# Two small loads and one matmul group of a two-block transformer kernel: packed loads issued early from GpSimd's queue become strided loads issued later from ScalarE's queue, and half-width matmuls become full-width

## The chip, the cores and the metric

One Trainium2 chip, one core. The kernel is one program that keeps its own weights, activations and intermediate results on that core. The metric is the device time of one execution in microseconds (us); lower is better. Times of matrices below are read from one profiled execution.

## The reference

A batch of one sequence of 256 rows with 2048 features goes through two transformer blocks, all in float32. The first block has gated linear attention, forgetting attention and attention to a memory, then an MLP. The second one, on which the change bears, begins with one wide projection and a sparse attention whose keys and values are first compressed, and with a pooling mixer beside it:

```
h = rms_norm_2(x, ln_mix_pre); z = h @ w_in                  # [256, 7728]
# compressed keys (kv = 0) and values (kv = 1), windows of 32 rows, stride 16, so 15 windows:
blk  = raw[:, idx] + cmp_pe[kv]                              # cmp_pe: [2, 32, 64]
kc/vc = gelu(flat(blk) @ cmp_w1[kv]) @ cmp_w2[kv]            # w1: [2048, 128], w2: [128, 64]
...
# pool mixer, per group g with trailing window w in (2, 4, 8, 16):
y = trailing_mean(u_g, w) - u_g ;  y = y @ w_pool[g] ;  y * pool_scale
```

Then come the merge of both branches, a cross-attention and a gated feed-forward, each with a norm behind it. The trailing mean of the pool mixer is computed as a product with a banded 256 x 256 matrix: column s1 of the band has entries only in the rows s0 with s1 - w < s0 <= s1 (less the identity), so the lower row block (rows 128 to 255) has nothing but zeros in columns 0 to 127.

## The kernel before

Each large product is made from float32 weights that are split in two parts. The work is cut into weight chunks of 1 MB (512 rows x 512 columns), which SyncE's queue (SP) loads into four slots `raw[:, c % SLOTS]`, line L336. A chunk is two halves q. For each half ScalarE rounds the weights into `whi` (function `hi`, line L563, engine ACT), VectorE makes the rest `wlo = raw - whi` (function `lo`, L1250, engine DVE), and TensorE (PE) makes 12 matmuls of 512 columns with them (function `half`, lines L2195, L2196, L2197) that stream into `ps_a`. `whi` and `wlo` have four places each.

The order is held by counters: `hi(q)` waits for `pe_half` >= q - 3 (TensorE is done with half q - 4), `lo(q)` waits for `hi_done`, `half(q)` waits for `lo_done`, and SP's load of chunk c + 4 waits for `lo_done` of chunk c's second half. So ScalarE may be up to four halves ahead of TensorE, and no more.

All other work of a stage is written by hand between the halves of the same engine program. In the second block's first projection (segment `in2`) each engine runs `for n in range(8, LAST2)`: one half, then `sparse(n)`, which holds what that engine does for the sparse attention and the pool mixer at half n. Halves 0 to 7 stand before the loop, mixed with the turned rows of the norm (`hi_group("n4", ...)`); behind them ScalarE has `square_sums(3)` (lines L670, L675: sums of squares of the 256 rows and a square root), and then the loop begins with `hi(q0 + 8)`.

Other places that matter:

- `pet` (the position embeddings `cmp_pe`) and `cw2` (the second compression weights, the first of them twice) are needed by VectorE's `windows` at n = 21 (L1891, writes `xpe`) and by TensorE after it (L2627, L2629). Both are loaded by one DMA each from GpSimd's queue (POOL), L1173 and L1174, from arrays that the host has laid out (`cmp_pe_t`, `cmp_w2_t`), near the start of the kernel. All their DMAs count on the semaphore `ld["cmp"]`.
- SP loads the first compression weights `cw1`, two DMAs of L418, when TensorE has done four halves of `in2`.
- At n = 68 TensorE multiplies `proj2` with `band` into `ps_b` (L2666): 8 values of x, 2 row blocks b. Row block 1 is multiplied with the columns 128 to 255 of its band alone. At n = 71 there is a product of the same form with `wpool` (L2675), of 16 matmuls with 256 columns. ScalarE and VectorE copy `ps_b` out to `yt` at n = 72.

The last chunk of the projection is a narrow one (`tail2`, 48 columns wide), loaded by one DMA of 2048 short rows.

Of the kernel before, what the change touches and what calls it, by code (L numbers as in the profile page):

```python
# [26 lines left out]
P = 128  # L27
S = 256
SB = S // P
# [26 lines left out]
NSA_H, NSA_G, HD2 = 16, 4, 64  # L56
# [3 lines left out]
NU = NGL + 3 * NSA_H  # L60
# [5 lines left out]
CMP_LEN, CMP_STRIDE = 32, 16  # L66
# [46 lines left out]
def hybrid_blocks_kernel(nc, a, c_base, c_bands, out):  # L113
    es = ExitStack()
    with es:
# [27 lines left out]
        proj2 = sb("proj2", [P, SB, IN2])  # L143
# [74 lines left out]
        band = sb("band", [P, SB, 4, S], at=free2 + 6144)  # L218
        wpool = sb("wpool", [P, 4, 2, S], at=free2 + row2 + 6144)
        pet = sb("pet", [P, 2, CMP_LEN // 2])  # L220
        cw2 = sb("cw2", [P, 3, HD2])
# [20 lines left out]
        ps_b = es.enter_context(nc.psum_tensor("ps_b", [P, 4 * NT], F32))  # L242
# [310 lines left out]
        def _(act):  # L553
# [102 lines left out]
            def square_sums(n):  # L656

                if n in (0, 1, 4):
                    for j in range(4):
                        act.wait_ge(norm_loaded[2 if n == 4 else n][j], 16)  # L660
                elif n == 2:
                    act.wait_ge(evicted, seg["mlp"][2])
                elif n == 3:
                    act.wait_ge(d_add, 64)
                else:
                    act.wait_ge(post_done, 8 * (n - 4))
                to = junk if n < 2 else junk_mix if n < 4 else junk3
                src = norms[n]
                for b in range(SB):
                    ins = nc.scalar.activation(to[:], src[:, b], ACT.Square, accum_out=s_sq[:, b:b + 1])  # L670
                    if b == 0:
                        link(ins)
                ins.then_inc(n_sq, 1)
                act.wait_ge(n_var, n + 1)
                nc.scalar.activation(s_std, s_var, ACT.Sqrt).then_inc(n_std, 1)  # L675
# [276 lines left out]
            hi_group("n4", 3, xhi)  # L952
            some("in2", 6, 8)
            square_sums(3)

            def branch_exps(x, t):
                act.wait_ge(nb["max"], 2 * x + t + 1)
# [193 lines left out]
        @block.gpsimd  # L1151
        def _(pool):
            def load_rows(n, rows_, src):
                for j in range(4):
                    c = slice(j * NT, (j + 1) * NT)
                    pool.dma_start(rows_[:, :, c], a[src][0].rearrange("(b p) d -> p b d", p=P)[:, :, c]).then_inc(norm_loaded[n][j], 16)

            def load_flat(n, src):
                for j in range(4):
                    c = slice(4 * j, 4 * j + 4)  # L1160
                    pool.dma_start(FLAT[n][0][:, c], a[src][:, c]).then_inc(flat_loaded[n][j], 16)

            pool.wait_ge(flat_loaded[0][1], 16)
            load_rows(0, mem_rows, "mem")

            pool.wait_ge(flat_lo, 8)
            load_flat(1, "x_t")
            pool.wait_ge(pe_half, 8)
            load_rows(1, h, "x")
            pool.wait_ge(pe_half, 16)  # L1170
            pool.dma_start(base[:, P:], c_base[:, P:]).then_inc(ld["base"], 16)

            pool.dma_start(pet[:], a["cmp_pe_t"]).then_inc(ld["cmp"], 16)  # L1173
            pool.dma_start(cw2[:], a["cmp_w2_t"]).then_inc(ld["cmp"], 16)  # L1174

            G = nc.gpsimd


            normed = (proj1[:, :, FQ:FQ + 512], proj1[:, :, FK:FK + 512], mkv[:, :, 0:512], proj1[:, :, MQ:MQ + 512])
            pool.wait_ge(hn["rstd"], 1)  # L1180
            for n, v in enumerate(normed):
                for b in range(SB):
                    rows_ = v[:, b].rearrange("p (h d) -> p h d", d=HD)
                    ins = G.tensor_tensor(rows_, rows_, s_hrstd[:, 8 * n + 4 * b:8 * n + 4 * b + 4].unsqueeze(2).to_broadcast([P, 4, HD]), ALU.mult)
                if n % 2:
                    ins.then_inc(hn["rows"], 1)

            pool.wait_ge(pe_half, seg["wout"][1])

            def distance(l):  # L1190
                w = LEVELS_ALL[l]
                if l >= 2:
                    pool.wait_ge(gla["q"], l - 1)
                    pool.wait_ge(gla["k"], l - 1)
                else:
                    pool.wait_ge(gla["b"], 1)
                v = gbt[:].rearrange("p x (m t) -> p (x m) t", t=2 * w)
                G.tensor_tensor(ge[:, l % 2].rearrange("p x (m t) -> p (x m) t", t=2 * w), v,
                                v[:, :, w - 1:w].to_broadcast([P, 4 * S // (2 * w), 2 * w]), ALU.subtract).then_inc(gla["d"], 1)

            distance(0)
            G.memset(gke[:], 0.0).then_inc(gla["zero"], 1)
            pool.wait_ge(gla["zero"], 1)
            for l in range(8):
                w = LEVELS_ALL[l]
                if l < 7:
                    distance(l + 1)
                pool.wait_ge(gla["e"], l + 1)
                if l >= 2:
                    pool.wait_ge(gla["s"], l - 1)  # L1210
                first = [t.rearrange("p x (m t) -> p (x m) t", t=2 * w)[:, :, 0:w] for t in (gke[:, l % 2], gkt[:], ge[:, l % 2])]
                G.tensor_tensor(*first, ALU.mult).then_inc(gla["k"], 1)


            pool.wait_ge(fx["rstd"], 1)
            pool.wait_ge(gate_done, 2)
            fox_mix = mix[:, :, FOX_AT:FOX_AT + 512]
            for b in range(SB):
                G.tensor_tensor(fox_mix[:, b].rearrange("p (h d) -> p h d", d=HD), fox_o[:, b].rearrange("p (h d) -> p h d", d=HD),
                                s_orstd[:, 16 * b + 8:16 * b + 12].unsqueeze(2).to_broadcast([P, 4, HD]), ALU.mult).then_inc(fx["over"], 1)  # L1220
            for b in range(SB):
                pool.wait_ge(fx["over"], b + 1)
                ins = G.tensor_tensor(fox_mix[:, b], fox_mix[:, b], proj1[:, b, FG:FG + 512], ALU.mult)
            ins.then_inc(fx["mixed"], 1)


            pool.wait_ge(t_ps, sum(QUADS["y1"]))
            load_rows(2, mix, "mem_2")
            pool.wait_ge(n_sq, 5)
            load_flat(2, "mem_2_t")  # L1230
# [3 lines left out]
        def _(dve):  # L1234
# [662 lines left out]
            def sparse(n):  # L1897
# [4 lines left out]
                    V.memset(kcbd[:], 0.0).then_inc(ns["zero"], 1)  # L1902
                if n == 21:
                    dve.wait_ge(ns["tk"], 1)
                    dve.wait_ge(ld["cmp"], 16 * 2)
                    windows(0)
                if n == 22:
                    windows(1)
# [272 lines left out]
        def _(pe):  # L2181
# [414 lines left out]
            def sparse(n):  # L2596
# [63 lines left out]
                if n == 68:  # L2660
                    pe.wait_ge(nb["y"], 1)
                    pe.wait_ge(evicted, seg["in2"][2] + 8)
                    pe.wait_ge(band_loaded, 16)
                    for x in range(8):
                        for b in range(SB):
                            ins = mm(ps_b[:, x * S + b * P:(x + 1) * S], proj2[:, b, NU + x * P:NU + (x + 1) * P],  # L2666
                                     band[:, b, x // 2, b * P:S], start=b == 0, stop=b == SB - 1)
                    ins.then_inc(ns["yps"], 1)
                if n == 71:
                    pe.wait_ge(ns["ysb"], 2)  # L2670
# [127 lines left out]


_INS = ["x", "mem", "w_in", "gla_a_w2", "fox_f_b", "w_mem_kv", "w_out", "w_up", "w_down", "mem_2", "ln_mix_post_2", "ln_x_post_2",  # L2800
        "ln_ffn_post_2", "w_in_2", "cmp_w1_2", "w_pool_2", "w_br_attn_2", "w_br_pool_2", "w_mix_out_2",
        "w_xq_2", "w_xkv_2", "w_xo_2", "w_gate_2", "w_up_2", "w_down_2"]


# [4 lines left out]
def laid_out(inputs, index):  # L2809

    flat = {n + "_t": np.asarray(inputs[n])[0].reshape(S, KB, P).transpose(2, 1, 0) for n in ("x", "mem", "mem_2")}
    flat["gains_t"] = np.concatenate([np.asarray(inputs[n]).reshape(-1, P) for n in _GAINS]).T
    table = np.concatenate([np.asarray(inputs["rel_bias_2"])[HEAD_ORDER], np.full((NSA_H, 1), NEG, np.float32)], 1)
    flat["bias"] = table[:, index].transpose(1, 0, 2)
    heads = np.array(HEAD_ORDER)
    kv = 1024 + (np.array(KIND_ORDER)[:, None] * 256 + np.arange(256)).ravel()
    q = (heads[:, None] * HD2 + np.arange(HD2)).ravel()
    gl = NGL + (heads[:, None] * 3 + np.arange(3)).ravel()
    flat["w_in_2"] = np.asarray(inputs["w_in_2"])[:, :, np.concatenate([kv, q, gl, np.arange(NU, IN2)])]
    flat["w_br_attn_2"] = np.asarray(inputs["w_br_attn_2"])[:, q]  # L2820
    flat["cmp_pe_t"] = np.asarray(inputs["cmp_pe_2"])[0].reshape(2, CMP_LEN // 2, P).transpose(2, 0, 1)
    flat["cmp_w2_t"] = np.asarray(inputs["cmp_w2_2"])[0][[0, 0, 1]].transpose(1, 0, 2)
    return {n: np.ascontiguousarray(v, np.float32) for n, v in flat.items()}


# [20 lines left out]
```

## Time and profile before

| | |
|---|---|
| time, median of 3 runs | 2561.34 us (2560.51 to 2563.33) |
| the profiled execution's own time | 2561.34 us |
| its span, first to last instruction | 2559.5 us |
| TensorE matmul busy | 2492.3 us (97%) |
| TensorE weight load busy | 2175.4 us (85%) |
| VectorE busy | 1570.6 us (61%) |
| ScalarE busy | 1209.5 us (47%) |
| GpSimd busy | 61.5 us (2%) |
| share of TensorE in the chain that ended last | 92% |
| mean granted TensorE clock | 0.988 |

The span is 1.84 us shorter than the execution's own time; that execution is the median one. A busy share is an average over stages. The chain that ended last is followed back from the last instruction, at each step to what released it; work that stands in it sets the time. "PEld" is TensorE's weight load, which runs beside its matmuls. "SPq" and "ACTq" rows are DMA issues on the sequencers of SyncE and ScalarE; their duration is the time for which the sequencer was held by the issue.

### The profile page before, as it was taken

To read this page: it belongs to the slowest core of one execution; us is meant where nothing else is said; L and a number is where in the kernel's file an instruction comes from. 1 tells how busy PE (TensorE), PEld (TensorE's weight loads), DVE (VectorE), ACT (ScalarE), POOL (GpSimd) and SP (SyncE) were. 2 spreads that over 40 slices of the span, in tenths; PEclk is the share of its full clock that TensorE was granted. 3 is DMA by queue.
4 is the path that set the end of the run, shared out by engine and by line. 5 is a ranking of instruction groups with operands and counts; after the bars stand their busy time and mean duration, and the time that the engine had idled before them with its cause. 6 is when DMAs were issued, how large, how long until landed. Compare 5 with 4: busy or idle time off the path is not lost.

```text
span 2559.5 us, 31690 instructions
## 1 busy us (share of the span) xinstructions
PE 2492.3 (97%) x12062; PEld 2175.4 (85%) x12062; DVE 1570.6 (61%) x1999; ACT 1209.5 (47%) x1516; POOL 61.5 (2%) x56
## 2 busy tenths in 40 slices
PE   8999988999999999999999999999899999999997
PEld 7888877888888888888888788888788888888886
DVE  6555777656565655566555666766555555555556
ACT  6444454544444444545344545565454444444443
POOL 1000240000000000000000000000000000000000
PEclk9999979999999999999999999999899999999999
DMA  9776405556565656556563445675356666666653
GB/s 369 217 209 198 150 1 191 188 197 202 192 210 185 212 185 208 190 204 228 175 205 132 155 133 196 206 270 183 130 197 198 199 203 202 199 200 203 203 197 115
DMA packets 244526, 488.72 MB, mean 191 GB/s; under 512 B 11928, under 2 KB 13240, under 8 KB 243672
## 3 DMA queue, kind: packets, MB, share of 16 engines
q1 hardware_dynamic: 240576, 470.42, 56.1%
q0 software_dynamic: 3104, 11.79, 1.2%
q10 hardware_dynamic: 760, 5.34, 0.5%
q8 instruction: 57, 0.93, 0.1%
q14 instruction: 29, 0.24, 0.0%
HBM read 485.42 MB, written 2.10 MB: 190 GB/s over the span
## 4 chain that ended last, share of the span: by engine, by line
PE 92%; DVE 3%; ACT 2%; issue 1%; DMA 1%; SPq 0%; DVEq 0%; ACTq 0%
PE ps_a L2195 24%; PE ps_a L2196 24%; PE ps_a L2197 24%; PE ps_b L2196 5%; PE ps_b L2197 5%; PE ps_b L2195 5%; DMA raw<-in_w_mem_kv 1%; PE ps_b L2501 1%; PE ps_b L2260 1%; DVE wlo L1250 1%; PE ps_b L2575 0%; ACT whi L563 0%; PE ps_b L2565 0%; DVE h L1435 0%; ACT prob L962 0%
## 5 line engine op out<-in xcount | busy, mean ns | idle before, releaser
L1250 DVE TENSOR_TENSOR wlo<-raw,whi 128x1024 fp32r<-128x1024 f32 x880 | 1067.8, 1222 | 727.2 <-ACT whi L563 726.1
L563 ACT CAST whi<-raw 128x1024 fp32r<-128x1024 f32 (+1 forms) x884 | 916.0, 1045 | 1065.0 <-PE ps_a L2197 829.4
L2195 PE MATMUL ps_a<-whi,xhi 128*128 128x512 f32 x2016 | 773.0, 383 | 8.8 <-DVE wlo L1250 6.3
L2196 PE MATMUL ps_a<-wlo,xhi 128*128 128x512 f32 x2016 | 766.9, 380 | 0.0
L2197 PE MATMUL ps_a<-whi,xlo 128*128 128x512 f32 x2016 | 766.4, 380 | 0.0
L2195 PEld LDWEIGHTS ps_a<-whi,xhi 128*128 128x128 f32 x2016 | 383.0, 190 | 67.1 <-issue 10.6
L2197 PEld LDWEIGHTS ps_a<-whi,xlo 128*128 128x128 f32 x2016 | 383.0, 190 | 54.0
L2196 PEld LDWEIGHTS ps_a<-wlo,xhi 128*128 128x128 f32 x2016 | 383.1, 190 | 52.2
L2195 PE MATMUL ps_a<-whi,x2hi 128*128 128x512 f32 x640 | 246.0, 384 | 11.5 <-DVE wlo L1250 11.5
L2196 PE MATMUL ps_a<-wlo,x2hi 128*128 128x512 f32 x640 | 243.7, 381 | 0.0
L2197 PE MATMUL ps_a<-whi,x2lo 128*128 128x512 f32 x640 | 243.5, 381 | 0.0
L2195 PEld LDWEIGHTS ps_a<-whi,x2hi 128*128 128x128 f32 x640 | 121.7, 190 | 29.3 <-issue 11.0
L2197 PEld LDWEIGHTS ps_a<-whi,x2lo 128*128 128x128 f32 x640 | 121.7, 190 | 17.2
L2196 PEld LDWEIGHTS ps_a<-wlo,x2hi 128*128 128x128 f32 x640 | 121.8, 190 | 16.6
L2195 PE MATMUL ps_b<-whi,uhi 128*128 128x512 f32 x352 | 133.6, 380 | 0.0
L2197 PE MATMUL ps_b<-whi,ulo 128*128 128x512 f32 x352 | 133.5, 379 | 0.0
L2196 PE MATMUL ps_b<-wlo,uhi 128*128 128x512 f32 x352 | 133.5, 379 | 0.0
L2195 PE MATMUL ps_a<-whi,muhi 128*128 128x512 f32 x272 | 103.4, 380 | 0.0
L2197 PE MATMUL ps_a<-whi,mulo 128*128 128x512 f32 x272 | 103.2, 379 | 0.0
L2196 PE MATMUL ps_a<-wlo,muhi 128*128 128x512 f32 x272 | 103.2, 379 | 0.0
L2196 PE MATMUL ps_b<-wlo,muhi 128*128 128x512 f32 x240 | 91.0, 379 | 0.0
L2197 PE MATMUL ps_b<-whi,mulo 128*128 128x512 f32 x240 | 91.0, 379 | 0.0
(327 smaller groups left out, 1957.2 us busy)
## 6 DMA issues: line engine op xcount, KB each, us to landing
raw<-in_w_in SPq DMA_DIRECT2D x108, 1024.0 KB, 5.3
raw<-in_w_up SPq DMA_DIRECT2D x108, 1024.0 KB, 5.3
raw<-in_w_down SPq DMA_DIRECT2D x108, 1024.0 KB, 5.1
raw<-in_w_gate SPq DMA_DIRECT2D x44, 1024.0 KB, 5.0
raw<-in_w_out SPq DMA_DIRECT2D x16, 1024.0 KB, 5.1
raw<-in_w_mix_out SPq DMA_DIRECT2D x16, 1024.0 KB, 5.7
raw<-in_w_br_attn SPq DMA_DIRECT2D x8, 1024.0 KB, 5.0
raw<-in_w_br_pool SPq DMA_DIRECT2D x8, 1024.0 KB, 5.0
```

The lines of the kernel that those rows point to most:

```text
L563: return nc.scalar.copy(o, i)
L1250: return V.tensor_tensor(wlo[:, q % 4], raw[:, c % SLOTS, 2 * j:2 * j + 2], whi[:, q % 4].bitcast(F32), ALU.subtract).then_inc(lo_done, 1)
L2195: mm(o, x0, m0, start=first and j == 0, stop=False)
L2196: mm(o, x0, m1, start=False, stop=False)
L2197: ins = mm(o, x1, m0, start=False, stop=last and j == len(kbs) - 1)
L2260: ins = nc.tensor.transpose(o[:, m * P:(m + 1) * P], src[:, b, (kb + m) * P:(kb + m + 1) * P], ident)
L2501: ins = nc.tensor.transpose(ps[:, (b * 4 + j) * P:(b * 4 + j + 1) * P], src[:, b, j * P:(j + 1) * P], ident)
```

## The change

Two things are changed.

1. `pet` and `cw2` are no longer loaded by GpSimd's queue, and the host makes no packed arrays. ScalarE's queue loads them from the reference's own arrays, behind `square_sums(3)` and before `hi(q0 + 8)`. `pet` takes four DMAs, one for each kv and each parity t of the row l: 64 partitions (the feature d) with 16 single float32 each, whose source addresses are 64 floats x 2 apart along l and 1 apart along d. `cw2` takes three DMAs of 128 partitions with 64 contiguous floats. VectorE's wait at n = 21 is for 7 DMAs in place of 2.
2. The band product at n = 68 multiplies row block 1 with all 256 columns of its band, in place of the last 128.

```diff
@@ scalar program, behind the first tile of in2
             some("in2", 6, 8)
             square_sums(3)
+            for kv in range(2):
+                for t in range(2):
+                    act.dma_start(pet[t * HD2:(t + 1) * HD2, kv], a["cmp_pe_2"][0, kv].rearrange("(l t) d -> t d l", t=2)[t],
+                                  allow_slow_non_contiguous=True).then_inc(ld["cmp"], 16)
+            for n, kv in enumerate((0, 0, 1)):
+                act.dma_start(cw2[:, n], a["cmp_w2_2"][0, kv]).then_inc(ld["cmp"], 16)
@@ gpsimd program
             pool.dma_start(base[:, P:], c_base[:, P:]).then_inc(ld["base"], 16)
 
-            pool.dma_start(pet[:], a["cmp_pe_t"]).then_inc(ld["cmp"], 16)
-            pool.dma_start(cw2[:], a["cmp_w2_t"]).then_inc(ld["cmp"], 16)
-
@@ vector program, sparse(n)
                 if n == 21:
                     dve.wait_ge(ns["tk"], 1)
-                    dve.wait_ge(ld["cmp"], 16 * 2)
+                    dve.wait_ge(ld["cmp"], 16 * 7)
                     windows(0)
@@ tensor program, sparse(n), n == 68
                         for b in range(SB):
-                            ins = mm(ps_b[:, x * S + b * P:(x + 1) * S], proj2[:, b, NU + x * P:NU + (x + 1) * P],
-                                     band[:, b, x // 2, b * P:S], start=b == 0, stop=b == SB - 1)
+                            ins = mm(ps_b[:, x * S:(x + 1) * S], proj2[:, b, NU + x * P:NU + (x + 1) * P], band[:, b, x // 2],
+                                     start=b == 0, stop=b == SB - 1)
@@ host
-    flat["cmp_pe_t"] = np.asarray(inputs["cmp_pe_2"])[0].reshape(2, CMP_LEN // 2, P).transpose(2, 0, 1)
-    flat["cmp_w2_t"] = np.asarray(inputs["cmp_w2_2"])[0][[0, 0, 1]].transpose(1, 0, 2)
```

(The list of inputs gains `cmp_pe_2` and `cmp_w2_2`.)

## Rows read from the trace of the kernel before

**Rows 1.** The profile's page: engines, and the chain that ended last by engine.

```profile
PE 2492.3 (97%) x12062; PEld 2175.4 (85%) x12062; DVE 1570.6 (61%) x1999; ACT 1209.5 (47%) x1516; POOL 61.5 (2%) x56
...
PE 92%; DVE 3%; ACT 2%; issue 1%; DMA 1%; SPq 0%; DVEq 0%; ACTq 0%
```

**Rows 2.** The chain in order of time: start us, length us, what (band, then wpool group).

```profile
1372.61 5.24 PE ps_b L2666 x32
...
1385.62 6.91 PE ps_b L2675 x32
```

**Rows 3.** ScalarE's timeline from 1174 to 1192 us: start, length, instruction [idle before].

```profile
1178.03 1.05 ACT L563 CAST whi<-raw 128x1024 fp32r<-128x1024 f32 x1 [0.95 <-PE ps_a L2197]
1178.98 1.91 ACT L670 ACTIVATE junk_mix<-h 128x2048 f32<-128x2048 f32 x1
...
1183.24 0.20 ACT L675 ACTIVATE small<-small 128x2 f32<-128x2 f32 x1 [0.24 <-DVE small L1340]
1183.35 1.98 ACT L563 CAST whi<-raw 128x1024 fp32r<-128x1024 f32 x2
1185.80 1.05 ACT L563 CAST whi<-raw 128x1024 fp32r<-128x1024 f32 x1 [0.46 <-PE ps_a L2197]
1188.38 1.05 ACT L563 CAST whi<-raw 128x1024 fp32r<-128x1024 f32 x1 [1.54 <-PE ps_a L2197]
```

**Rows 4.** VectorE's timeline, 1184 to 1190 us, and its first use of `pet`.

```profile
1184.48 3.62 DVE L1250 TENSOR_TENSOR wlo<-raw,whi 128x1024 fp32r<-128x1024 f32 x3 [0.84 <-ACT whi L563]
1188.33 1.41 DVE L1849 TENSOR_SCALAR proj<-ps_a,small 128x512 f32<-128x512 f32 x2 [0.23 <-PE ps_a L2197]
...
1216.51 2.73 DVE L1891 TENSOR_TENSOR xpe<-ps_b,pet 64x240 f32<-64x240 f32 x8
```

**Rows 5.** ScalarE's timeline, 70 to 76 us: two DMA issues and what follows.

```profile
70.98 0.20 ACT L675 ACTIVATE small<-small 128x2 f32<-128x2 f32 x1 [0.24 <-DVE small L1340]
70.99 0.34 ACTq L771 DMA_DIRECT2D gw<-in_gla_a_w  x1
71.37 0.57 ACTq L772 DMA_DIRECT2D fbias<-in_fox_f_b  x1
72.04 2.94 ACT L563 CAST whi<-raw 128x1024 fp32r<-128x1024 f32 x3 [0.85 <-issue]
```

**Rows 6.** SyncE's queue, 1180 to 1190 us: the issues around the `cw1` loads.

```profile
1180.36 0.37 SPq L336 DMA_DIRECT2D raw<-in_w_in  x1
1180.93 4.71 SPq L418 DMA_DIRECT2D cw<-in_cmp_w  x2
1186.87 2.58 SPq L336 DMA_DIRECT2D raw<-in_w_in  x1
```

**Rows 7.** The two issues of line L418 alone: ns min/median/max, and their landing.

```profile
L418 SPq MOVE_SHAPE cw<-in_cmp_w x2: 122/244/366, 1180.8 to 1181.8; - x2
L418 SPq DMA_DIRECT2D cw<-in_cmp_w x2: 833/2128/3422, 1180.9 to 1182.2; - x2
...
DMA to landing us min/median/max: 8.6/9.8/10.9
```

**Rows 8.** DMA from 1496 to 1500 us: the narrow tail's one load.

```profile
DMA packets 2064, 0.39 MB, mean 98 GB/s; under 512 B 2064, under 2 KB 2064, under 8 KB 2064
...
raw<-in_w_in SPq DMA_DIRECT2D x1, 384.0 KB, 3.4
```

**Rows 9.** Stretches: length, engines' busy us, PEclk, DMA share, GB/s.

```profile
330.00:340.00 10.00, 5.22 (x23) 4.70 (x22) 8.72 (x23) 6.86 (x20) 5.48 (x3) 0.50 0.00 0
...
1180.00:1190.00 10.00, 10.00 (x48) 8.78 (x47) 5.92 (x9) 7.17 (x9) 0.00 (x0) 1.00 0.88 266
1190.00:1200.00 10.00, 10.00 (x48) 8.75 (x47) 4.54 (x4) 5.94 (x8) 0.00 (x0) 1.00 1.03 351
1200.00:1216.00 16.00, 16.00 (x84) 14.20 (x83) 9.47 (x11) 6.51 (x7) 0.00 (x0) 1.00 0.60 201
```

**Rows 10.** The timelines of GpSimd and ScalarE at the two removed issues.

```profile
56.20 0.55 POOL L1173 DMA_DIRECT2D pet<-in_cmp_pe_t  x1
56.74 0.55 POOL L1174 DMA_DIRECT2D cw<-in_cmp_w_t  x1
288.86 4.89 POOL L1184 TENSOR_TENSOR proj<-proj,small 128x512 f32<-128x512 f32 x4 [231.57 <-DVE small L1549]
...
53.89 1.05 ACT L563 CAST whi<-raw 128x1024 fp32r<-128x1024 f32 x1 [0.44 <-DMA raw<-in_w_in]
```

**Rows 11.** ScalarE's timeline, when it reaches half 16 of `in2`.

```profile
1201.34 1.05 ACT L563 CAST whi<-raw 128x1024 fp32r<-128x1024 f32 x1 [1.10 <-PE ps_a L2197]
```

More of the change, by code:

```diff
@@ L2800 @@
 _INS = ["x", "mem", "w_in", "gla_a_w2", "fox_f_b", "w_mem_kv", "w_out", "w_up", "w_down", "mem_2", "ln_mix_post_2", "ln_x_post_2",
-        "ln_ffn_post_2", "w_in_2", "cmp_w1_2", "w_pool_2", "w_br_attn_2", "w_br_pool_2", "w_mix_out_2",
+        "ln_ffn_post_2", "w_in_2", "cmp_pe_2", "cmp_w1_2", "cmp_w2_2", "w_pool_2", "w_br_attn_2", "w_br_pool_2", "w_mix_out_2",
         "w_xq_2", "w_xkv_2", "w_xo_2", "w_gate_2", "w_up_2", "w_down_2"]
```

## The prediction

> **What bounds the kernel now.** I read the page first. The reader is to see there that TensorE's matmuls are busy 97% of the span and make 92% of the chain that ended last [rows 1]. So a microsecond added to TensorE's own work is a microsecond of time, while an added microsecond elsewhere counts only if it empties what TensorE has in store. Then I went to the two places that the change touches: the chain in order of time at the band product [rows 2], and the timelines of ScalarE, VectorE and SyncE's queue where the new issues will stand [rows 3, 4, 6]. What an issue costs its sequencer I took from ScalarE's own issues and SyncE's [rows 5 to 8], and how full the DMA engines are from a table of stretches [rows 9].
>
> **Part 1, the band product.** In the chain the band group of 32 instructions (two passes for each of 16 matmuls) holds 5.24 us, and the group with `wpool`, also 32 instructions, all with 256 columns, holds 6.91 us [rows 2]. The changed band group has that form: same count, same widths. So it costs 6.91 - 5.24 = 1.67 us more. It lies in the chain and nothing hides it. The copies to `yt` that wait for it come 1.67 us later, but in that time TensorE isn't consuming halves either, so their distance stays. Part 1 is worth +1.67 us, and I see no bound far from that; the row for comparison stands 13 us later in the same stage.
>
> **Part 2, what is removed.** Two issues on GpSimd's queue at 56.2 us, 0.55 us each, of 112 KB together by their shapes (128 x 32 and 128 x 192 floats). GpSimd's next work stands at 288.86 us, released by VectorE, and ScalarE's wait for a weight chunk before 53.89 us lies ahead of them [rows 10]. Nothing waits behind them: 0. Their bytes at 351 GB/s [rows 9] would be 0.3 us of DMA, which bounds a gain.
>
> **Part 2, what is added on ScalarE.** Seven DMA issues stand in ScalarE's order between the square root at 1183.24 us and `hi` of half 8, which now starts at 1183.35 us [rows 3]. Behind them are queued half 8's `hi`, then VectorE's `lo`, then TensorE's half 8. ScalarE has no idle time there that they could fill. How long may half 8 be late? VectorE starts its `lo` at 1184.48 us, 1.13 us after `hi` starts; three of them take 3.62 us, so the first is done at about 1184.48 + 1.23 = 1185.71 us. TensorE ends half 7 at about 1188.3 us, when VectorE's copy of that tile starts [rows 4]. The store is 1188.3 - 1185.7 = 2.6 us. It is so small because `square_sums(3)` has already eaten the rest: with the usual cadence `hi` of half 8 would have started 2.7 us earlier, by two steps of 2.59 us before half 10's at 1185.80 [rows 3]. For half 9 and later the store is larger, since ScalarE takes 1.05 us for a half and TensorE 2.59. So the price is (time of the seven issues) - 2.6 us, paid once, and TensorE doesn't get it back.
>
> Time of the seven issues. The trace has no DMA with single floats 512 bytes apart. From below: issues on ScalarE's own queue held it 0.34 and 0.57 us, and 1.05 us from the first issue to the next `hi` [rows 5]; the 0.57 was for a load of 4 single floats. At 0.41 us each with its gap, seven are 2.9 us. A load of 2048 short rows was issued in the 0.37 us of any chunk and landed in 3.4 us [rows 8], so on an idle queue many descriptors don't hold the issuer. From above: the second `cw1` issue held SyncE's queue 3.42 us [rows 7] and the chunk behind it 2.58 us [rows 6]. By these, 4 x 3.42 + 3 x 2.58 = 21.4 us. These two are nearer to the case for one reason: ScalarE would issue at 1183.3 us, when SyncE's queue is itself stuck in the second `cw1` issue (to 1185.64 us) and soon in the next one (1186.87 to 1189.45), with the DMA engines at 0.88 and then 1.03 of their time [rows 6, 9]. `cw1` is 2 x 128 x 16 = 4096 rows of 512 bytes, and its issues held the queue from 1180.8 to 1185.64 us, 4.8 us, shape setting included. The four `pet` loads are 4 x 64 x 16 = 4096 single floats. I take the same 4.8 us for them, 0.4 us for two more shape settings (0.12 to 0.37 us each [rows 7]), and 3 x 0.41 = 1.2 us for `cw2`: 6.4 us, say 6.5. Late by 6.5 - 2.6 = 3.9 us. If bytes and not pieces set the time it is less (112 KB against `cw1`'s 2 MB); if the pieces take turns with SyncE's packets it is more.
>
> The Trainium skill, page "DMA: Bandwidth & Descriptors", section "Rules for kernel authors", speaks against this part: a strided last dimension is lowered to one descriptor per element, so `pet` would be 4096 descriptors in place of 128 rows. The trace agrees as far as it reaches: the narrow tail's 2048 rows show as 2064 packets [rows 8]. The same page (section "Bandwidth") gives about 10.5 ns for a small packet; as an estimate from that, 4096 of them over 16 engines are 2.7 us of DMA time, which is under the 2.9 us of seven bare issues and would leave the sum at its low end.
>
> What else could be late. The chunk issued at 1186.87 us is needed by ScalarE for half 16 at 1201.34 us [rows 6, 11]; at the slowest landing near here, 10.9 us [rows 7], it is there at 1197.8 with 3.5 us left, and a stall of TensorE moves its due time out as well. VectorE's wait for the seven loads comes at 1216.5 us [rows 4], 33 us behind the issues; the same slowest landing is a third of that. Both are hidden: 0.
>
> **Sum.** 2561.34 (the profiled execution's own time, also the median of the runs) + 1.67 + 3.9 = 2566.9 us, 0.22% more. A difference of under about 0.2% (5.1 us) can't be told from none in a measurement of this kernel; the forecast lies at that bound.
>
> **Rivals.**
> - *Cheap issues.* The queue takes the descriptors without holding ScalarE: 2.9 to 3.6 us for seven, late by 0.3 to 1.0 us, total +2.0 to +2.7, about 2563.7 us. For it: the tail's 0.37 us [rows 8] and ScalarE's 0.34 [rows 5]. Against it: none of those was issued into a full queue, the `cw1` issues were [rows 7].
> - *ScalarE held until the backlog is gone.* Single floats take turns with SyncE's 2 KB packets, and the later issues wait for room. The engines stay full up to 1200 us [rows 9], though with TensorE standing SyncE gets no new slot and its last megabytes are through by about 1195. ScalarE held from 1183.3 to between 1190 and 1195: 6.7 to 11.7 us, late by 5.5 at the middle (8.1 held) and 9.1 at the far end, total +7.2 to +10.8, about 2570 us; the bound from above, 21.4 us held, would be +20.5.
> - *The issues cost nothing*, because the sequencer runs them beside the square root and half 8 has more store than I read: +1.7, 2563.0 us. Against it: the 0.85 us that ScalarE idled behind two issues [rows 5].
> - *Faster.* TensorE's clock falls to half (0.50, the 1.2 GHz level) from 330 to 340 us, where it is busy about half of the time [rows 9]. If the earlier traffic, now without two loads, shifted that stretch so that the fall came late, 10 us at half clock would give back up to 5 us; to win it must exceed the 5.6 us above plus 5.1, so two such stretches. Nothing in the change reaches there: GpSimd's next work waits for VectorE, not for these loads.
>
> **Chances.** Forecast as worked out (total +3.8 to +7.0, so 2565.1 to 2568.3): 0.40. Cheap issues 0.27, backlog 0.25, nothing but the band 0.05, faster than the band's cost allows 0.03 (0.02 of it past 0.2%). Of the forecast's 0.40, about 0.25 lies above 5.1 us; with the backlog's 0.25 that is 0.50 slower by over 0.2%; 0.48 within; 0.02 faster. The range goes down to 2563.0 (band alone) and up to 2573.0, which takes in the backlog's far end and leaves the issue bound out, under 1 in 10.
>
> **What the changed profile would show.** Right: the band group at 6.9 us in the chain; seven ACTq issues from about 1183.3 us with `hi` of half 8 near 1189.8; TensorE idle for about 4 us before its half 8, released by VectorE's `wlo`; SyncE's next chunk issues later by the same; no wait of VectorE at its first `xpe`. Cheap issues would show ACTq rows of 0.4 us and an idle of under 1 us. Backlog would show rows of 2 to 6 us from the second or third issue on, and longer SPq rows beside them. The prediction is wrong if TensorE also waits for a weight chunk near half 16, if `xpe` starts late, or if the clock falls behind the stall at 1188 us.

## The result, and the profile after

The changed kernel takes 2574.95 us (median of 5, 2573.84 to 2576.09) against 2561.59 us for the kernel before (median of 5 beside it): 13.4 us more, ratio 1.0054 with a 95% interval of 1.0043 to 1.0066, or 11 to 17 us. It is slower, and outside the predicted range, whose upper end was 2573.0.

The page of the changed kernel, in the lines that answer to [rows 1]: the matmuls are as busy as before (2493.1 against 2492.3 us), so the added time is no work of TensorE's. The chain now holds a share of VectorE that is 4% and not 3, and a queue of ScalarE's (ACTq) appears in it.

```profile
PE 2493.1 (97%) x12062; PEld 2171.2 (84%) x12062; DVE 1570.0 (61%) x1999; ACT 1209.6 (47%) x1516; POOL 60.4 (2%) x54
...
PE 92%; DVE 4%; ACT 2%; issue 1%; DMA 1%; ACTq 0%; SPq 0%; DVEq 0%
```

The chain in order of time (start, length, what) shows both parts of the change. The first lines stand where [rows 3] had the square root and then `hi` of half 8 at once; the last two answer to [rows 2].

```profile
1181.42 0.51 ACTq L957
...
1181.96 0.79 ACTq L957
...
1182.78 4.12 ACTq L957
...
1186.92 0.70 ACTq L957
...
1187.66 4.09 ACTq L960
...
1191.79 0.45 ACTq L960
...
1192.27 0.45 ACTq L960
...
1192.82 1.05 ACT whi L563
...
1193.96 1.24 DVE wlo L1253
...
1195.34 0.76 PE ps_a L2198
1196.10 0.43 PE ps_a L2199
...
1382.67 6.91 PE ps_b L2669 x32
...
1397.35 6.91 PE ps_b L2678 x32
```

L957 are the four `pet` loads, L960 the three `cw2` loads (the lines behind the new ones are 3 to 6 higher than before; L2198 to L2200 are the three matmuls of `half`). From the first issue to `hi` of half 8 there are 11.4 us, and two of the seven issues hold 8.2 of them. Only then come `whi`, `wlo` and TensorE's half 8. The waits of that stretch (who waited for whom, us in total, times, longest) name it:

```profile
ACT whi L563 <- issue: 11.4, 1, 11.4
...
PE ps_a L2198 <- DVE wlo L1253: 9.1, 1, 9.1
```

The matmuls of half 8 follow each other in 0.43 us and not in 0.22. The table of stretches says why (the column behind the five engines is the granted clock; 0.50 is the level of 1.2 GHz):

```profile
1188.00:1190.00 2.00, 0.00 (x0) 0.00 (x0) 0.00 (x0) 0.00 (x0) 0.00 (x0) 1.00 1.09 269
1190.00:1192.00 2.00, 0.00 (x0) 0.00 (x0) 0.00 (x0) 0.00 (x0) 0.00 (x0) 0.68 1.14 150
1192.00:1194.00 2.00, 0.00 (x0) 0.00 (x0) 0.04 (x1) 1.18 (x2) 0.00 (x0) 0.50 0.25 49
1194.00:1196.00 2.00, 0.67 (x2) 0.61 (x3) 2.00 (x2) 2.00 (x3) 0.00 (x0) 0.50 0.02 4
1200.00:1202.00 2.00, 2.00 (x8) 1.63 (x8) 0.04 (x1) 1.04 (x1) 0.00 (x0) 0.76 0.88 234
```

TensorE stood from 1186.3 us on, its clock fell during that idle time, and it came back only at about 1201 us. The chain gives 5.83 us to the first 13 matmuls behind the idle time, the 12 of half 8 and one of half 9 (0.76 + 11 x about 0.43 + 0.37). At full speed they would take about 0.45 + 12 x 0.216 = 3.04 us, the 0.45 being what a first matmul behind an idle takes in runs below where the clock stayed up. So the fallen clock costs 2.8 us in this execution.

The account of this stage: 9.07 us idle and 2.8 us of slow matmuls make 11.9 us. Measured from ScalarE's last `whi` before `square_sums(3)` (1178.03 before, 1176.00 after) to the band group (1372.61 and 1382.67), the stage is 10.06 + 2.03 = 12.1 us longer. The 0.2 us between the two is the first matmul behind the idle, 0.45 us in place of 0.22. The band group adds 6.91 - 5.24 = 1.67 us, as forecast. That is 13.8 us. The 2.03 us by which the profiled execution of the changed kernel was ahead at 1176 us isn't the change's: of the change, only the two loads that no longer issue at 56 us lie ahead of that point, and in e2 below, where they are gone as well, the same `whi` starts at 1178.75 us. With that lead, 13.8 - 2.0 = 11.8 us are left, about what the two profiled executions differ by (2573.28 and 2561.34 us). The lead was there already at 495 us; before that lies a stretch in which the granted clock differs between the two executions (0.60 and 0.50 before, 0.69 and 0.63 after, in the stretches 320 to 330 and 330 to 340 us).

### The profile page after: what moved, and what is told of

It is laid out like the page before. It is cut to its first block, busy times and chain, and to the rows that moved or that the text cites. A ratio compares the mean times of both kernels' runs of the same rounds, so it can differ in the third digit from the quotient of the medians.

```text
span 2571.5 us, 31695 instructions
## 1 busy us (share of the span) xinstructions
PE 2493.1 (97%) x12062; PEld 2171.2 (84%) x12062; DVE 1570.0 (61%) x1999; ACT 1209.6 (47%) x1516; POOL 60.4 (2%) x54
## 3 DMA queue, kind: packets, MB, share of 16 engines
q1 hardware_dynamic: 240576, 470.42, 56.8%
## 4 chain that ended last, share of the span: by engine, by line
PE 92%; DVE 4%; ACT 2%; issue 1%; DMA 1%; ACTq 0%; SPq 0%; DVEq 0%
PE ps_a L2198 24%; PE ps_a L2199 23%; PE ps_a L2200 23%; PE ps_b L2200 5%; PE ps_b L2199 5%; PE ps_b L2198 5%; DMA raw<-in_w_mem_kv 1%; PE ps_b L2504 1%; PE ps_b L2263 1%; DVE wlo L1253 1%; ACT whi L563 1%; PE ps_b L2578 0%; PE ps_b L2568 0%; DVE h L1438 0%; ACT prob L968 0%
## 5 line engine op out<-in xcount | busy, mean ns | idle before, releaser
L2198 PE MATMUL ps_a<-whi,xhi 128*128 128x512 f32 x2016 | 774.3, 384 | 17.9 <-DVE wlo L1253 15.4
L2200 PE MATMUL ps_a<-whi,xlo 128*128 128x512 f32 x2016 | 767.2, 381 | 0.0
L2198 PEld LDWEIGHTS ps_a<-whi,xhi 128*128 128x128 f32 x2016 | 383.3, 190 | 77.4 <-issue 20.0
L2200 PEld LDWEIGHTS ps_a<-whi,xlo 128*128 128x128 f32 x2016 | 382.9, 190 | 55.1
L2198 PE MATMUL ps_a<-whi,x2hi 128*128 128x512 f32 x640 | 246.0, 384 | 11.3 <-DVE wlo L1253 11.3
L2200 PE MATMUL ps_a<-whi,x2lo 128*128 128x512 f32 x640 | 243.6, 381 | 0.0
L2198 PEld LDWEIGHTS ps_a<-whi,x2hi 128*128 128x128 f32 x640 | 121.7, 190 | 29.4 <-issue 10.8
L2200 PEld LDWEIGHTS ps_a<-whi,x2lo 128*128 128x128 f32 x640 | 121.7, 190 | 17.5
L2198 PE MATMUL ps_b<-whi,uhi 128*128 128x512 f32 x352 | 133.5, 379 | 0.0
L2200 PE MATMUL ps_b<-whi,ulo 128*128 128x512 f32 x352 | 133.4, 379 | 0.0
L2198 PE MATMUL ps_a<-whi,muhi 128*128 128x512 f32 x272 | 103.3, 380 | 0.0
L2200 PE MATMUL ps_a<-whi,mulo 128*128 128x512 f32 x272 | 103.1, 379 | 0.0
L2198 PE MATMUL ps_b<-whi,muhi 128*128 128x512 f32 x240 | 91.0, 379 | 0.0
```

Source lines behind the costliest of these rows:

```text
L2198: mm(o, x0, m0, start=first and j == 0, stop=False)
L2200: ins = mm(o, x1, m0, start=False, stop=last and j == len(kbs) - 1)
```

## The experiments

Theory H, formed on these rows: an issue of ScalarE's own queue is held when two strided loads are already pending on it, and it is held long because their single floats share the DMA engines with SyncE's two `cw1` loads. Rivals: a fixed price by the element on the issuing sequencer (E); the place, where SyncE's queue is itself stuck (P), or the place in ScalarE's program or the stage (S); the number of loads (N); single floats that hurt the DMA engines wherever they are issued (D). All experiments but the first keep the band product as before. "Held" is the wait of ScalarE's first `whi` behind the issues; TensorE's idle is its wait for `wlo` before the half behind them. "More" is the difference of the two medians in us, with what I expected by H in brackets.

| run | what | median us | before, same chip | more (expected) | ratio (95% interval) | held | TensorE idle |
|---|---|---|---|---|---|---|---|
| e1_band_only | band alone | 2564.87 | 2561.58 | 3.3 (1.7) | 1.0012 (1.0003 to 1.0021) | - | - |
| e2_loads_only | loads alone | 2574.88 | 2561.58 | 13.3 (11.5 to 12.5) | 1.0052 (1.0039 to 1.0066) | 11.5 | 9.1 |
| e3_packed_on_act | 2 packed loads, ScalarE | 2561.50 | 2561.58 | -0.1 (0) | 1.0001 (0.9992 to 1.0010) | 0.9 | 0 |
| e4_behind_sums2 | 7 loads, a stage earlier | 2565.81 | 2561.58 | 4.2 (2 to 4) | 1.0017 (1.0007 to 1.0026) | 4.7 | 2.7 |
| e5_cw1_later | 7 loads, `cw1` moved away | 2565.42 | 2561.80 | 3.6 (2.5 to 4.5) | 1.0015 (1.0006 to 1.0024) | 4.6 | 2.2 |
| e6_whole_rows | 7 loads without single floats | 2562.82 | 2561.80 | 1.0 (0.5 to 1.5) | 1.0002 (0.9993 to 1.0011) | 4.0 | 1.7 |
| e8b_pet_only | 4 strided loads | 2567.31 | 2562.15 | 5.2 (4, or 6 to 7) | 1.0025 (1.0016 to 1.0034) | 6.7 | 4.4 |
| e10_cw2_first | 7 loads, other order | 2572.03 | 2562.15 | 9.9 (5 to 9) | 1.0044 (1.0030 to 1.0058) | 9.7 | 7.4 |
| e11_cw1_long_rows | `cw1` in 2 KB rows | 2570.17 | 2560.93 | 9.2 (11 to 13, or 3 to 7) | 1.0036 (1.0022 to 1.0051) | 9.6 | 7.3 |
| e9_at_half_17 | 7 loads at half 17 | 2562.20 | 2562.15 | 0.1 (0 to 0.5) | 1.0002 (0.9993 to 1.0011) | 4.2 | 0 |
| e7b_strided_on_pool | 8 strided loads and 3 plain, GpSimd | 2562.34 | 2562.15 | 0.2 (0 to 1) | 0.9999 (0.9990 to 1.0008) | - | - |

e7 and e8, the first forms of e7b and e8b, gave no time.

**The parts by themselves.** e1 has only the four changed lines of the band product, e2 all of the change but them.

> Only the band product is changed; the two packed loads stay on GpSimd's queue. If the parts add up, the band group of 32 takes 6.9 us in the chain in place of 5.24 and the kernel is 1.7 us slower, ratio 1.0007. If full-width matmuls bring some further wait (ScalarE or VectorE late behind the copy to yt), it is above +3 us.

> Only the loads are changed; the band product is as before. Theory H (ScalarE's issues are held): TensorE idles about 9 us before half 8 and runs some 6 us at half clock behind it, +11.5 to +12.5 us in all, ratio 1.0047. If the two parts work on each other, the two changes alone don't sum to the +13.4 us of both.

The loads alone give 13.3 us, with an interval of 10 to 17 us, the band alone 3.3 us, with an interval of 0.8 to 5.4 us. Their sum is 16.6 and not 13.4 us, but the intervals are too wide to tell that the parts work on each other. The chain of e1 has the two groups at 6.91 us each, and ScalarE's copy behind the group waits 5.81 us for it, as it waits for the `wpool` group:

```profile
1374.35 6.91 PE ps_b L2666 x32
...
1389.03 6.91 PE ps_b L2675 x32
```

So the group itself costs 1.67 us. A further cost of one or two microseconds isn't excluded by the medians. The profiled execution of e1 does lose another 1.7 us, but ahead of the group: it starts at 1374.35 us where it had started at 1372.61, with the stage begun within 0.1 us of before. The stretches of e1 show it, in the form of [rows 9]:

```profile
1300.00:1305.00 5.00, 5.00 (x30) 4.50 (x30) 3.63 (x6) 0.09 (x1) 0.00 (x0) 0.79 0.63 202
1305.00:1310.00 5.00, 5.00 (x22) 4.28 (x21) 1.99 (x3) 1.56 (x2) 0.00 (x0) 0.87 0.17 65
```

TensorE is busy the whole time; behind a group of 32 narrow matmuls (32 columns each, L2644) its clock falls, and about eight matmuls of 512 columns take 0.43 us and not 0.22. The same fall, worth the same 1.7 us, stands in nine of the thirteen profiled executions, e1 to e6, e8b, e10 and e11, and not in the kernel before, the changed one, e9 and e7b. e3 has it with a median equal to the kernel before's, so it belongs to the execution and not, as far as the runs show, to an edit; what decides it stays open. So a median of few runs can be off by a difference of this size, and the held and idle times are the surer rows below.

**Place or pieces?** e3 issues the packed loads of the kernel before from the new place.

```diff
             square_sums(3)
+            act.dma_start(pet[:], a["cmp_pe_t"]).then_inc(ld["cmp"], 16)
+            act.dma_start(cw2[:], a["cmp_w2_t"]).then_inc(ld["cmp"], 16)
```

> The two packed loads of the kernel before (same bytes, 128 long rows each) issued from ScalarE's queue at the changed kernel's place, into the same cw1 traffic; band as before. Theory H (the number of pieces fills ScalarE's queue): two issues of about 0.4 to 0.5 us, under the 2.6 us in store, so 0 us, 2561.6. Rival P (the place is what costs: ScalarE can't issue while SyncE's queue is stuck in cw1): the first or second issue is held 2 to 4 us and the kernel is 0 to 3 us slower. Far over that neither.

ScalarE's timeline in e3; SyncE's `cw1` issues held its own queue until 1184.98 us:

```profile
1182.81 0.36 ACTq L955 DMA_DIRECT2D pet<-in_cmp_pe_t  x1
1183.21 0.56 ACTq L956 DMA_DIRECT2D cw<-in_cmp_w_t  x1
1183.86 2.94 ACT L563 CAST whi<-raw 128x1024 fp32r<-128x1024 f32 x3 [0.85 <-issue]
```

The same bytes from the same place cost nothing. ScalarE issued both loads while SyncE's queue was stuck in its own issue, so that alone doesn't hold ScalarE's: P falls.

**Traffic or element?** e4 has the seven loads behind `square_sums(2)`, where no `cw1` is in flight. e5 leaves them at the new place and moves `cw1`:

```diff
-            sp.wait_ge(pe_half, seg["in2"][1] + 4)
+            linear("in2", 2, 4)
             for kv in range(2):
                 sp.dma_start(cw1[kv][:], ...).then_inc(cw1_loaded[kv], 16)
-            linear("in2", 2, 6)
+            linear("in2", 4, 6)
```

> The seven new loads unchanged, but issued one stage earlier, behind square_sums(2) at about 503 us, where ScalarE is just as short of store (about 2.5 us) and SyncE loads only its weight chunks, no cw1; band as before. Theory H with traffic (pieces take turns with cw1's): ScalarE is held 4 to 6 us, TensorE idles 1.5 to 3.5 us, +2 to +4 us. Rival E (a fixed price by the element on the sequencer, whatever the traffic): held 11.5 us as before, TensorE idle about 9 us, +11 to +12 us. If the price is the bare issue, held 3 to 3.6 us, +0.5 to +1.

> The seven new loads stay where the change puts them; what is moved is the traffic: SyncE issues its two cw1 loads behind the weight chunks of two more tiles (up to its chunk of half 31) and not when half 4 of in2 is done. Band as before. Theory H (the third issue waits for room because the pieces of the first two take turns with cw1's): ScalarE is held 4.8 us as it was behind square_sums(2), TensorE idles about 2.7 us, no fall of its clock, +2.5 to +4.5 us against the kernel before, and 9 to 11 us less than with the loads alone. Rival S (the place in ScalarE's program, or the stage, costs): held 11.5 us as before, +13 us. Later cw1 could itself be late for TensorE near half 28: that would show as a wait on a DMA there.

Both have the same picture. ScalarE's timeline of e5:

```profile
1183.15 2.98 ACTq L957 DMA_DIRECT2D pet<-in_cmp_pe  x4
1186.18 1.64 ACTq L960 DMA_DIRECT2D cw<-in_cmp_w  x3
1187.91 3.90 ACT L563 CAST whi<-raw 128x1024 fp32r<-128x1024 f32 x4 [4.55 <-issue]
```

With `cw1` gone, no issue is held: four strided ones in 2.98 us and three plain ones in 1.64. The landing of the `pet` loads (us min/median/max), first in e5 and then in the changed kernel, is the other side of it:

```profile
DMA to landing us min/median/max: 2.7/2.9/2.9
```

```profile
DMA to landing us min/median/max: 6.1/8.5/10.5
```

E and S fall: 4.6 us are the price of seven issues without `cw1`, and 6.8 of the 11.4 us come from its traffic. The DMA engines weren't free in e5 either; the end of one weight chunk was in flight. These are the stretches of the third strided issue, first in e5 (0.70 us) and then in the changed kernel (4.12 us):

```profile
1184.60:1185.30 0.70, 0.70 (x5) 0.62 (x4) 0.00 (x0) 0.00 (x0) 0.00 (x0) 1.00 1.03 108
```

```profile
1182.78:1186.90 4.12, 3.48 (x17) 2.71 (x15) 0.00 (x0) 0.00 (x0) 0.00 (x0) 1.00 1.13 272
```

The engines are as full in one as in the other (1.03 and 1.13). What differs is how much SyncE's queue still moved meanwhile, 108 against 272 GB/s. So a busy share doesn't tell whether an issue will be held.

**Pieces or loads?** e6 has the seven loads in `cw1`'s traffic, with contiguous runs of 16 floats.

```diff
-   act.dma_start(..., a["cmp_pe_2"][0, kv].rearrange("(l t) d -> t d l", t=2)[t], ...)
+   act.dma_start(..., a["cmp_pe_2"][0, kv].rearrange("l (c e) -> (l c) e", e=16)[t * HD2:(t + 1) * HD2])
```

> The same seven loads at the same place, with cw1's traffic, but each pet load reads 64 whole rows of 16 contiguous floats in place of 64 x 16 single ones (same bytes and count of loads; pet then holds other values). Band as before. Theory H (pieces count): no issue is held beyond 0.4 to 0.6 us, seven take 3.0 to 3.8 us, TensorE idles 0.4 to 1.2 us, +0.5 to +1.5 us. Rival N (the number of loads in flight is what SyncE's backlog blocks): the third and fifth issue are still held 4 us, +13 us.

```profile
1183.00 2.48 ACTq L957 DMA_DIRECT2D pet<-in_cmp_pe  x4
1185.52 1.58 ACTq L959 DMA_DIRECT2D cw<-in_cmp_w  x3
```

No issue is held, so N falls, and the holding needs both single floats and traffic. Even so seven issues took 4.0 us and not the 3.8 at most of the expectation: all but the first cost 0.45 to 0.62 us, not 0.41.

**How the room is used.** e8b has the four `pet` loads only (`cw2` packed on GpSimd's queue); e10 has `cw2`'s three loads ahead of `pet`'s four.

> Only the four strided pet loads from ScalarE at the new place, in cw1's traffic; cw2 stays packed on GpSimd's queue, with a counter of its own. Band as before. From the changed kernel's rows (0.5 + 0.8 + 4.1 + 0.7 us): ScalarE held 6.4 us, TensorE idles about 3.9 us. If the clock keeps full speed after so short an idle, +4 us; if it falls as after 9 us, +6 to +7 us. Theory H says that the 4.1 us of the first cw2 load was the wait for pet's pieces, not cw2's own price.

> The seven new loads at the new place in cw1's traffic, band as before; only their order is turned: the three cw2 loads first, then the four pet loads. Theory H (an issue waits when two strided loads are already pending): 3 x 0.45 to 0.7 for cw2, then 0.7 + 0.8 + about 4 + 0.7 for pet, nothing left to be held behind it: 7.5 to 8.5 us held, TensorE idles 5 to 6 us, 3.5 us less idle than in the change's order, and the clock's fall smaller or gone: +5 to +9 us. Rival E2 (each of the seven costs what it cost, in any order): 11.5 us held, +13 us.

The chain of e8b, and then that of e10:

```profile
1182.07 0.50 ACTq L957
...
1182.61 0.79 ACTq L957
...
1183.43 4.52 ACTq L957
...
1187.98 0.70 ACTq L957
```

```profile
1182.64 0.70 ACTq L959
...
1183.37 0.80 ACTq L959
...
1184.20 5.35 ACTq L959
...
1189.58 1.36 ACTq L959
```

The third strided load is held each time, 4.1 to 5.4 us. In the change's order ScalarE is held a second time, at the first `cw2` load, 4.09 us for a load that costs 0.67 elsewhere; put ahead, all three cost 1.3 us. The order alone saves 1.7 us of holding against e2, less than the 3.5 that I expected, since the third and fourth strided loads then take longer (5.35 and 1.36 us), and e10 is slower than my range. H is not exact either: the fourth strided load goes in 0.70 us in the change's order and in e8b. In e8b TensorE idled 4.4 us, and its clock fell even so.

**What of the traffic counts?** e11 reads `cw1`'s two megabytes as rows of 2 KB, a quarter of the pieces. `cw1` then holds other values.

```diff
-   sp.dma_start(cw1[kv][:], a["cmp_w1_2"][0, kv].rearrange("(l p) n -> p l n", p=P))...
+   sp.dma_start(cw1[kv][:].rearrange("p (k m) n -> p k (m n)", m=4), rows(w1["in2"], kv * 512, 512, 0))...
```

> The seven new loads at the new place, band as before, and SyncE's two cw1 loads at their time and with their 1 MB each, but read as rows of 2 KB (512 rows of another matrix per load) in place of 2048 rows of 512 bytes; cw1 then holds other values. If it is SyncE's bytes in flight that hold ScalarE's issues, they are held about as long as before (11.5 us, +11 to +13 us). If it is the number of SyncE's pieces that the single floats take turns with, ScalarE is held 5 to 8 us and the kernel is +3 to +7 us. With no effect of the traffic's form or amount beyond a running chunk load it would be 4.8 us and +3.

From e11's chain, the third and fourth strided loads:

```profile
1182.28 3.47 ACTq L957
...
1185.78 3.02 ACTq L957
```

Held 9.6 us: between my two branches and nearer to the one of bytes. Here the third and the fourth are held, and the first `cw2` load isn't (0.67 us). With `cw1` in long rows 1.8 of the 6.8 us go and 5.0 stay. That the rest comes from the amount in flight is likely, but argued: no run changed the amount alone.

**Where it costs nothing.** e9 issues the seven loads behind half 17, e7b from GpSimd's queue at the old place.

```diff
@@ scalar program, sparse(n)
+                if n == 17:
+                    ... the seven loads of the change ...
```

> The seven new loads issued behind half 17 of in2, at about 1205 us, when ScalarE has its full store (a half may be late by about 5.3 us there) and cw1 has landed; VectorE needs them at about 1216 us. Band as before. Theory H: ScalarE held 4.6 to 4.8 us, half 18's rounding 3.3 us late, within the store; TensorE doesn't idle; 0 to +0.5 us, 2561.6 to 2562.1. If an issue that holds ScalarE always costs TensorE: +2 us or more. If the loads land too late for VectorE: a wait at the first xpe.

> The strided loads issued from GpSimd's queue at the old place (56 us), pet in eight loads of 32 partitions in place of four of 64 (11 loads in all); ScalarE's program is as before; band as before. Theory H (only the issuer that others wait for matters): GpSimd may be held for long, nobody waits, 0 to +1 us, 2561.6 to 2562.6. Rival D (4096 single-float pieces hurt the DMA engines in the full first stage): TensorE waits for a weight chunk near 60 to 80 us, +2 us or more.

ScalarE's timeline in e9, and VectorE's:

```profile
1202.43 2.98 ACTq L977 DMA_DIRECT2D pet<-in_cmp_pe  x4
1205.44 2.12 ACTq L980 DMA_DIRECT2D cw<-in_cmp_w  x3
1207.66 2.00 ACT L563 CAST whi<-raw 128x1024 fp32r<-128x1024 f32 x2 [4.20 <-PE ps_a L2201]
...
1214.99 2.73 DVE L1895 TENSOR_TENSOR xpe<-ps_b,pet 64x240 f32<-64x240 f32 x8
```

ScalarE's sequencer is in the issues for 5 us in all, half 18's rounding starts 2.7 us behind its place, and TensorE has no wait in that stretch: 0.05 us between the medians. `xpe` follows `wlo` without a gap. In e7b GpSimd's eight strided issues stretch from 56.8 to 91.0 us, and nobody waits; ScalarE's waits for weight chunks between 50 and 120 us add up to 2.4 us, against 2.6 before, so D falls. In e9 too the engines were full during the third issue (a share of 1.14, at 157 GB/s).

## Why the prediction was wrong

- *Part 1, +1.67 us*: right, 6.91 us in the chain.
- *Removed loads, 0*: right. Nothing waits near 56 us, and e3 and e7b show that either queue can carry them at no cost.
- *The store of 2.6 us*: right within 0.3 us. In all six runs at that place where TensorE had to wait (and in the changed kernel), its idle is ScalarE's held time less 2.3 to 2.4 us: 11.4 to 9.1, 9.7 to 7.4, 9.6 to 7.3, 6.7 to 4.4, 4.6 to 2.2, 4.0 to 1.7. e3's 0.9 us disappeared in it.
- *Time of the seven issues, 6.5 us*: this step failed; it was 11.4 us. I took the time that SyncE's queue was held by 4096 rows of `cw1` as the time for 4096 single floats, as if ScalarE's queue had the DMA engines to itself. The runs showed two terms in its place: 4.6 us for the issues proper (strided 0.5 to 0.8 us, plain 0.45 to 0.67 [rows 5 had 0.34 and 0.57]), and 6.8 us of waiting for room while `cw1` was under way, which is there only with single floats and this traffic together (e5, e6).
- *What I left out*: the clock. The sum had no term for it; it stood only among the things that would make the prediction wrong. It was put at nothing without a reason, and cost 2.8 us in the profiled execution, and by the same count 1.4 in e2's, 1.6 in e10's, 1.7 in e8b's and 2.0 in e11's. With idle times of 9.1, 7.4, 7.3 and 4.4 us the clock was at 0.50 for the first matmuls behind them; with 2.7, 2.2 and 1.7 us it stayed at 1.00.
- *The rival "held until the backlog is gone"* was the right mechanism, with a chance of 0.25. Its far end, 9.1 us late, is what TensorE idled. Its total of +10.8 us lacks the clock's 2.8 us, and with them is 13.6 us; that this meets the 13.4 us so closely is partly luck, as the clock's cost differs by 1.4 us between executions. One of its signs didn't come: SyncE's `cw1` issues took no longer (4.54 us against 4.71 in [rows 6]). *Cheap issues* is what would have happened without `cw1`: even then the loads alone are +3.6 us by e5's medians, where the rival had +2.0 to 2.7 with the band. *Costs nothing* holds at another place (e9). *Faster*: no sign of it.
- *Weight chunk near half 16, and VectorE's wait for the loads, both 0*: right. VectorE's first `xpe` stands at 1226.57 us, 10.06 us behind its time in [rows 4], as all of the stage.

The Trainium skill, page "DMA: Bandwidth & Descriptors", section "Issuing engines are not separate DMA queues", says that DMAs of all queues interleave on the same 16 engines. Here that agrees: `pet`'s loads, on another queue than `cw1`, landed in 8.5 us in its traffic and in 2.9 us without it. The section also says that the sequencer's time for an issue is usually small beside the DMA; for these seven loads it was 4.6 us even without `cw1`, and decided the result. The 2.7 us of DMA time that I had estimated by that page's figure are borne out (in e4 the 4592 packets of ScalarE's queue, nearly all of them single floats, took 13.7% of 20 us, which is 2.7 us), but say nothing of the time in which ScalarE is held.

What stays open: what the "room" is (pieces pending, loads pending, or both). The third strided load is held in each order while `cw1` is under way, the fourth only in e11, and a load of 64 short pieces isn't; more than that the runs don't fix. Nor did I separate the amount of SyncE's traffic from its time.

None of the versions beats the kernel before. If the host isn't to pack the two arrays, e9 and e7b do without it in the same time; with the changed kernel's placing it costs 13 us.

## What to carry to other kernels

A DMA issue is an instruction of the engine that issues it. Before one is put into the program of an engine that feeds the critical one, read how late that engine already is there, and what is in flight on the DMA engines at that moment: the same seven loads cost 13 us beside `cw1`, about 4 us without it, and nothing 20 us later in the same program, and in smaller loads from a queue that nobody waits for they cost nothing either. Loads of single elements were what the queue had no room for here, so a packed layout, a queue that nobody waits for, or a place with a full store should carry them. And where a stall of several microseconds on TensorE is forecast, add a term for its clock behind it, from rows like these.

## What of the hardware was not expected

- A strided issue of 1024 single floats held ScalarE 0.70 us with room in the queue, one of 64 runs of 64 bytes 0.62 us, a plain one of 128 rows 0.45 us (0.67 where it followed the strided ones). So the element count itself costs the sequencer little; what it costs is room.
- The third such issue was held 3.5 to 5.4 us while SyncE's `cw1` loads were under way, and took 0.7 to 1.0 us in e4, e5 and e9 with the end of one chunk in flight (108 to 171 GB/s). The DMA engines were full in both cases (share 1.0 to 1.1).
- TensorE's clock fell to 0.50 (1.2 GHz) while it idled for 9.1 and 7.4 us, and at the end of an idle of 4.4 us, and the half behind it began slowly. The kernel before has a granted clock of 1.00 in that stage.
- In nine of the thirteen profiled executions the clock also fell for about eight matmuls at a place where TensorE was busy all the time, behind 32 matmuls of 32 columns (e1: 0.79 and 0.87 in the stretches above), and cost 1.7 us.
